# Experts of a mixture layer: gate and up columns in two passes with the gather between, sums after the next down products

## What is computed

```
logits = h @ router_w + router_b                 # 32 experts
top_vals, top_idx = top_k(logits, 4); gates = softmax(top_vals)
# per expert e, for the tokens that chose it:
gu   = x @ w_gu[e] + b_gu[e]                      # 1024 -> 2048: gate, up
gate = min(gu[:, :1024], 7);  up = clip(gu[:, 1024:], -7, 7)
y    = ((up + 1) * gate * sigmoid(1.702 * gate)) @ w_down[e] + b_down[e]
out[token] += gates[token, e] * y
```

## Time and profile before

| | us |
|---|---|
| three runs, median (lowest, highest) | 1225.59 (1220.59, 1228.70) |
| the profiled execution, its own time | 1226.34 |
| its span in the trace | 1224.4 |
| PE busy | 1032.1 (84%) |
| DVE, ACT, POOL busy | 378.8, 173.7, 127.2 |
| read from HBM | 455.56 MB |
| granted TensorE clock, mean | 0.95 |

### The profile page before, as it was taken

The page is one execution under the profiler, slowest core; times in us unless marked ns, Lnnn a source line. Parts: engine busy times, 40 slices in busy tenths (PEclk is TensorE's granted clock), DMA queues, the critical chain, the costliest instruction groups (busy, mean ns, idle before and its releaser), DMA issues.

```text
span 1224.4 us, 31651 instructions
## 1 busy us (share of the span) xinstructions
PE 1032.1 (84%) x11996; PEld 502.7 (41%) x11997; DVE 378.8 (31%) x1102; ACT 173.7 (14%) x459; POOL 127.2 (10%) x325
## 2 busy tenths in 40 slices
PE   5899988998999869898579899898765799989974
PEld 4678766646433314334123334333221233334331
DVE  1045592865222203223122231321211122222223
ACT  2242313142001001001000001000000010001002
POOL 0041103100101101001000010110100011000100
PEclk9899997997999989999879999999888899999998
DMA  9936937899999999999999995999999999999997
GB/s 340 338 138 226 351 94 201 319 312 393 384 426 427 427 429 428 428 428 429 428 429 429 428 400 216 429 429 429 428 428 428 430 428 429 428 429 429 428 428 298
DMA packets 77831, 463.68 MB, mean 379 GB/s; under 512 B 11531, under 2 KB 31185, under 8 KB 53146
## 3 DMA queue, kind: packets, MB, share of 16 engines
q1 hardware_dynamic: 70479, 460.88, 91.8%
q10 hardware_dynamic: 7315, 2.27, 0.9%
HBM read 455.56 MB, written 7.57 MB: 378 GB/s over the span
## 4 chain that ended last, share of the span: by engine, by line
PE 60%; DMA 17%; DVE 9%; SPq 6%; issue 5%; ACT 1%; DVEq 1%; ACTq 0%; POOLq 0%; POOL 0%
PE psum L655 26%; PE psum L671 13%; DMA weights<-in_w_gu 12%; PE psum L1011 4%; PE psum L630 3%; DMA work<-in_w_down 3%; SPq L898 3%; PE psum L1262 2%; PE psum L608 2%; PE psum L624 2%; DMA weights<-in_w_ada 2%; SPq L901 2%; PE psum L1016 2%; DVE work L2384 1%; PE psum L966 1%
## 5 line engine op out<-in xcount | busy, mean ns | idle before, releaser
L655 PE MATMUL psum<-weights,work 128*32 128x512 f32 x2928 | 357.1, 628 | 94.9 <-DMA weights<-in_w_gu 59.0
L655 PEld LDWEIGHTS psum<-weights,work 128*32 128x32 f32 x2928 | 93.1, 113 | 325.0 <-issue 237.2
L2384 DVE STREAM_TRANSPOSE work<-psum 128x256 f32<-128x256 f32 x53 | 23.9, 450 | 562.8 <-PE psum L655 562.8
L671 PE MATMUL psum<-weights,work 128*32 128x256 f32 x2624 | 152.8, 381 | 21.5 <-ACT work L1812 19.8
L671 PEld LDWEIGHTS psum<-weights,work 128*32 128x32 f32 x2624 | 80.4, 110 | 87.0 <-issue 35.2
L608 PE MATMUL psum<-work 128*32 128x257 f32 (+3 forms) x1296 | 91.5, 397 | 1.1 <-ACT work L1755 1.1
L1807 ACT ACTIVATE work<-work x53 | 22.1, 416 | 493.3 <-DVE work L2388 478.2
L1011 PE MATMUL psum<-work,weights 128*128 128x288 f32 x320 | 81.7, 412 | 0.0
L608 PEld LDWEIGHTS psum<-work 128*32 128x32 f32 (+1 forms) x1296 | 38.8, 112 | 70.8 <-issue 61.2
L1011 PEld LDWEIGHTS psum<-work,weights 128*128 128x128 f32 x320 | 60.3, 192 | 17.9 <-issue 2.0
L655 PE MATMUL psum<-work 128*32 128x512 f32 x464 | 58.7, 624 | 6.6 <-DMA work<-in_w_gu 6.6
(11 more groups left out here) (404 smaller groups left out, 921.9 us busy)
## 6 DMA issues: line engine op xcount, KB each, us to landing
weights<-in_w_gu SPq DMA_DIRECT2D x112, 2048.0 KB, 35.1
weights<-in_w_down SPq DMA_DIRECT2D x48, 2048.0 KB, 37.1
work<-in_w_gu SPq DMA_DIRECT2D x16, 2048.0 KB, 33.3
work<-in_w_down SPq DMA_DIRECT2D x16, 2048.0 KB, 40.5
weights<-in_w_ada SPq DMA_DIRECT2D x12, 2048.0 KB, 12.4
weights<-in_w_in SPq DMA_DIRECT2D x6, 2048.0 KB, 13.2
weights<-in_w_out SPq DMA_DIRECT2D x2, 2048.0 KB, 8.0
out<-weights SPq DMA_DIRECT2D x8, 512.0 KB, 9.9
```

The lines of the kernel that those rows point to most:

```text
L655: last = mm(bank(GB)[SLOTS * n:SLOTS * n + SLOTS, :].rearrange("p (a x) -> p a x", a=4), xTm[:, k, :], gu[:, k % 2, n], start=k == 0, stop ...
L671: last = mm(bank(YB)[SLOTS * q:SLOTS * q + SLOTS, 0:QW], hT[:, k, :], dn[:, k % 4, QW * q:QW * q + QW], start=k == 0, stop=k == KT - 1)
L2384: v.transpose(features, of_slots[0]).then_inc(s["hid_step"], 1)
```

## The change

In the first loop the products are made in two passes over k: the 1024 gate columns into bank 2, then `gather(i + 1)`, then the 1024 up columns into bank 3 (`UB`). DVE takes the gate half as soon as `gate_ps` says so, transposes the first half of the gathered tokens once the up pass has read k-tiles 0 to 3 (`gu_read`), and does the second half after the up half's transpose. `gu_read` now counts in the up pass alone.

In the second loop the down products (into bank 2) come first and `scatter(i)` behind them. `scatter` reads a copy `y_st`, which DVE makes from `y_sb` after the transpose of `selT`; the copy has the place of `b_down_sb`, so the products of b_down with the gates are moved before the first expert's second loop. ACT copies the *next* round's `hid` to the fixed place before it evicts a round; the first round is there already, so the first down products wait for `hid` alone, and `hidc` goes.

```diff
+        hid_next = M.at(E0 + 1536, NB + 1, KT * SLOTS)
+        y_st = b_down_sb
...
-            XB, GB, YB = 0, 2, 3
+            XB, GB, UB, YB = 0, 2, 3, 2
...
                 pe.wait_ge(s["sel"], i)
+                pe.wait_ge(s["xTm"], i - 1)
                 pe.wait_ge(s["gslot"], i - 1)
                 gather_by(selA, GC).then_inc(s["xg_ps"], 1)
...
-                pe.wait_ge(s["y_sb"], i)
+                pe.wait_ge(s["y_st"], i)
...
+                    pe.wait_ge(s["y_sb"], first)
                     pe.wait_ge(s["xTa"], i)
-                    for k in range(KT):
-                        if k % 2 == 0:
-                            gu = slot_gu(landed(k // 2)).rearrange("p j (a n x) -> p j n a x", a=4, n=NQ)
-                        if k == KT // 2:
-                            pe.wait_ge(s["xTm"], i)
-                        for n in range(NQ):
-                            last = mm(bank(GB)[SLOTS * n:SLOTS * n + SLOTS, :].rearrange("p (a x) -> p a x", a=4), xTm[:, k, :],
-                                      gu[:, k % 2, n], start=k == 0, stop=k == KT - 1)
-                        if k in (1, 3, 5):
-                            last.then_inc(s["gu_read"], 1)
-                    last.then_inc(s["gu_ps"], 1)
-                    gather(i + 1)
+                    for part in range(2):
+                        out = bank((GB, UB)[part])
+                        for k in range(KT):
+                            if k % 2 == 0:
+                                at = landed(k // 2) if part == 0 else slot_of(r, k // 2)[0]
+                                gu = slot_gu(at).rearrange("p j (a n x) -> p j n a x", a=4, n=NQ)
+                            if part == 0 and k == KT // 2:
+                                pe.wait_ge(s["xTm"], i)
+                            for n in range(NQ):
+                                last = mm(out[SLOTS * n:SLOTS * n + SLOTS, 0:QW].rearrange("p (a x) -> p a x", a=2), xTm[:, k, :],
+                                          gu[:, k % 2, n, 2 * part:2 * part + 2], start=k == 0, stop=k == KT - 1)
+                            if part and k in (1, 3, 5):
+                                last.then_inc(s["gu_read"], 1)
+                        last.then_inc(s["gu_ps" if part else "gate_ps"], 1)
+                        if part == 0:
+                            gather(i + 1)
+
+                if of:
+                    bias_products()
 
                 with pe.Fori(first, end) as i:
 
-                    scatter(i)
-                    pe.wait_ge(s["hidc"], i)
+                    pe.wait_ge(s["y_sb"], i)
+                    pe.wait_ge(s["xTa"], end)
+                    pe.wait_ge(s["hid"], i)
...
                     last.then_inc(s["y_ps"], 1)
+                    scatter(i)
+
+            def bias_products():
...
+                    act.wait_ge(s["hid"], last)
+                    act.wait_ge(s["y_ps"], i)
+                    act.copy(hid_all[:, 0, :], hid_next[:, round_behind(i, first), :].rearrange("p r n -> p (r n)"))
                     act.wait_ge(s["xg_ps"], 1)
-                    act.wait_ge(s["y_ps"], i)
-                    fn(y_sb, bank(3)[:, 0:QW], ACT.Identity, scale=gslot[:, round_of(i, first)]).then_inc(s["y_sb"], 1)
+                    act.wait_ge(s["y_st"], i)
+                    fn(y_sb, bank(2)[:, 0:QW], ACT.Identity, scale=gslot[:, round_of(i, first)]).then_inc(s["y_sb"], 1)
...
-                    v.wait_ge(s["gu_ps"], i)
+                    v.wait_ge(s["gate_ps"], i + 1)
+                    v.wait_ge(s["y_sb"], first)
                     v.transpose(features, of_slots[0]).then_inc(s["hid_step"], 1)
                     v.wait_ge(s["hid_step"], i * 5 + 1)
                     tt(kept.rearrange("p (k t) -> p k t", k=KT), part, bias[0], ALU.add).then_inc(s["hid_step"], 1)
                     v.wait_ge(s["hid_step"], i * 5 + 2)
                     ts(kept, kept, LIMIT, None, ALU.min).then_inc(s["g_ready"], 1)
+                    v.wait_ge(s["xg_ps"], i + 1)
+                    v.wait_ge(s["gu_read"], i * 3 + 2)
+                    x_half(0).then_inc(s["xTa"], 1)
+                    v.wait_ge(s["gu_ps"], i)
                     v.transpose(features, of_slots[1]).then_inc(s["hid_step"], 1)
-                    v.wait_ge(s["xg_ps"], i + 1)
-                    x_transposes()
+                    x_half(1).then_inc(s["xTm"], 1)
...
+                    v.wait_ge(s["y_sb"], i + 1)
+                    v.tensor_copy(y_st, y_sb).then_inc(s["y_st"], 1)
```

More of the change, by code:

```diff
@@ L184 @@
  wout_in wpool_in x1 x1_st x2T_ps xT_ps xTm x_in xg_ps xn xn2 y_ps y_sb z_sb cur gslot rank_b selT bgu_in
- bguT ahead xTa hidc curb """.split()
+ bguT ahead xTa y_st curb """.split()
 def build(nc, x_prompt, x_sample, c_prompt, c_sample, state_pool, state_conv, state_ssm, w_ada, b_ada,
@@ L587, in round_of, with round_behind @@
             return bass.ds(r, 1)
+        def round_behind(i, first):
+            r = nc.s_assert_within(i - first + 1, 1, NB, skip_runtime_bounds_check_because="288 tokens are at most nine rounds of 32")
+            return bass.ds(r, 1)
         def slot_of(e, j):
@@ L623, in scatter @@
                     r = slice(SLOTS * q, SLOTS * q + SLOTS)
-                    last = mm(samples_out[r, :], selT[r, 0:SLOTS], y_sb[r, :], start=False, stop=end)
+                    last = mm(samples_out[r, :], selT[r, 0:SLOTS], y_st[r, :], start=False, stop=end)
                 if end:
@@ L629, in scatter @@
                         r = slice(SLOTS * q, SLOTS * q + SLOTS)
-                        last = mm(total(q, c), selT[r, SLOTS + P * c:SLOTS + P * c + P], y_sb[r, :], start=False, stop=end and c == 1)
+                        last = mm(total(q, c), selT[r, SLOTS + P * c:SLOTS + P * c + P], y_st[r, :], start=False, stop=end and c == 1)
                 last.then_inc(s["total_ps"], 1)
@@ L675, in expert @@
                     last.then_inc(s["y_ps"], 1)
+                    scatter(i)
+            def bias_products():
+                pe.wait_ge(s["gbT"], 1)
+                pe.wait_ge(s["rb_in"], 16 * NQ)
+                for c in range(2):
+                    for q in range(NQ):
+                        r = slice(NE * q, NE * q + NE)
+                        mm(total(q, c), gT[r, span(c)], b_down_sb[r, :], start=False, stop=False)
+                for q in range(NQ):
+                    r = slice(NE * q, NE * q + NE)
+                    mm(samples_out[r, :], gT[r, span(2)], b_down_sb[r, :], start=False, stop=False)
             pe.wait_ge(s["h2"], 3)
@@ L710, in experts_pe @@
             expert(0, 0, of_first)
-            pe.wait_ge(s["rb_in"], 16 * NQ)
-            for c in range(2):
-                for q in range(NQ):
-                    r = slice(NE * q, NE * q + NE)
-                    mm(total(q, c), gT[r, span(c)], b_down_sb[r, :], start=False, stop=False)
-            for q in range(NQ):
-                r = slice(NE * q, NE * q + NE)
-                mm(samples_out[r, :], gT[r, span(2)], b_down_sb[r, :], start=False, stop=False)
             for r in range(1, PERIOD):
@@ L2329, in _ @@
             v.wait_ge(s["bguT"], 1)
-            v.memset(y_sb, 0.0).then_inc(s["y_sb"], 1)
+            v.memset(y_sb, 0.0).then_inc(s["y_st"], 1)
             v.wait_ge(s["h2_ps"], 3)
```

18 lines of the change are left out of this document (9 added, 9 removed).

## The result

The changed kernel takes 1227.28 us (median of 18 runs, 1225.77 to 1232.86); the kernel before takes 1222.51 us (18 runs, 1220.16 to 1230.98) beside it. The ratio is 1.0038, interval 1.0027 to 1.0050: 4.8 us slower by the medians. That is inside the range of 1218 to 1234, but the forecast was 1.2 us faster, and the sign is wrong beyond the interval.

What follows compares the result with a forecast made beforehand. The experts' stage was taken as bound by its loads, so the end moves with the holes and the tail: -5.5 + 4.3 = -1.2 us, from the median 1225.6 to 1224.4 us; range 1218 to 1234.

Steps and rivals of the forecast that it cites:

- the sum of the holes: Dry times of the load stream around the first and five-round experts: 16.0 against 21.5 us, 5.5 us gained.
- the third hole: Load stream dry after 730, until the five-round expert's first w_down slot is free: 5.2 us instead of 15.0.
- the base: One profiled execution of the kernel before, 1226.34 us, supplied the rows; the forecast time started from the median, 1225.6 us.
- PE's stretch: PE's work from 631.32 to 756.03, through the five-round expert: starts 6.8 us late, gains 12.4 us.
- the place behind the third hole: Next expert's first w_gu slot: free at about 760.2, needed at 760.25, so nothing runs dry (0 to 1 us).
- the tail: After the last w_gu load: ACT begins 2.3 us later, the last sum adds 2.0; 4.3 us lost.
- The first hole: Load stream dry at the first expert's start: first reload 4.9 us later, 9.2 us dry instead of 4.3.
- PE's costs: PE's time per round: first loop 8.42 us instead of 9.38, second loop 5.14 instead of 6.18.
- The rival that the turns don't shorten: None of the eleven loop turns gains: +9.8 us, 1235.4 us; decides if a turn gains under 0.9 us; chance 0.15.
- The loop overhead: Jump back at the loop turns, taken as 0; at the other end 5.5 us over eleven turns.
- PE's start behind L: Next round's start after the load landing at 625.23 before: 8.05 us behind that load, 6.8 us late.
- The rival on the clock: Half clock behind the loads at PE's stretch and the tail: +7.1 us, 1231.5 us; chance 0.15.

Runs made afterwards that it cites:

- first expert in one pass: The changed kernel, but the first expert alone takes gate and up columns in one pass over k, gather behind: 1223.17 us, ratio 1.0000.
- both ends in one pass: The changed kernel with first and last expert in one pass, the last with its sum ahead of its down products: 1218.51 us, ratio 0.9964.
- passes alone: The kernel before with gate pass, gather, up pass, but its old second loop, down products in bank 3: 1230.35 us, ratio 1.0065.
- sums alone: The changed kernel with gate and up in one pass everywhere and DVE's old first-loop order, keeping the new second loop: 1220.19 us, ratio 0.9980.
- late reloads: The kernel before, its first three reloads waiting for all of the first expert's gate and up products: 1228.53 us, ratio 1.0042.
- sums, last expert as before: The changed kernel with one pass everywhere, DVE's old first-loop order, and the last expert's sum ahead of its down products: 1219.13 us, ratio 0.9966.
- last expert kept busy: The changed kernel with extra repeated gate products between the last expert's loads, which also waits for all gathered tokens: 1227.45 us, ratio 1.0041.

## Why the forecast was wrong, point by point

**The step that failed** is the sum of the holes: "5.5 us gained", with nothing lost behind the third. Measured from S against typical traces of before, the last w_gu load used comes only 0.2 us sooner (S + 892.2 for 892.4): the third hole ends 2.0 us sooner and the place behind it takes 1.7 of that back. With a tail near its forecast the sum is positive. Four terms make up the way from the forecast -1.2 to the +4.2 us of the traces:

- the base: its one trace was 2.4 us slow up to the end of the third hole;
- PE's stretch: it gains 10.45 us and not 12.4, 1.95 less, while it starts 0.8 us less late than summed, so 1.1 us;
- the place behind the third hole, taken at 0: 1.7 us;
- the tail: 0.2 us.

All traces, from S. The typical before is the mean of its three later traces; its first trace, which the sum was made from, stands apart.

| trace | first reload | L | third hole ends | tail | span - S | median, us over before |
|---|---|---|---|---|---|---|
| before, the sum's base | 3.0 | 320.6 | 451.4 | 25.0 | 919.8 | |
| before, three later traces | 2.6 | 320.1 | 449.05 | 25.0 | 917.4 | 0 |
| after, three traces | 8.1 | 325.5 | 447.1 | 29.5 | 921.6 | +4.8 |
| first expert in one pass | 2.7 | 320.1 | 442.8 | 29.9 | 918.3 | +0.6 |
| both ends in one pass | 3.7 | 321.4 | 443.1 | 25.3 | 913.8 | -4.0 |
| passes alone | 8.0 | 325.3 | 454.0 | 27.9 | 925.5 | +7.8 |
| sums alone | 3.1 | 320.9 | 446.3 | 26.3 | 916.4 | -2.4 |
| late reloads | 9.0 | 326.6 | 455.6 | 25.1 | 924.1 | +5.1 |
| sums, last expert as before | 3.5 | 320.9 | 446.2 | 25.2 | 916.0 | -4.3 |
| last expert kept busy | 8.2 | 325.6 | 448.6 | 28.0 | 921.5 | +5.2 |

**The whole, closed.** From the typical before to after: the third hole ends 2.0 us sooner, the place behind it, where the next expert's first w_gu slot comes free, takes about 1.7 back, and the tail costs 4.5. That is +4.2 us from S, and the medians say +4.8. The forecast had -5.5 and +4.3.

**The first hole: right.** Forecast: first reload 4.9 us later. It went 8.0 us after S instead of 3.0, and L came 4.8 us later than in the sum's base, 5.4 later than in typical traces. Late reloads shows that this lateness is carried to the end: 6.5 us at L, 6.5 at the third hole, 6.7 at the end.

**PE's costs: nearly right.** A first-loop round takes 725.67 - 717.20 = 8.47 us (forecast 8.42, have 9.38), a second-loop round 734.36 - 729.15 = 5.21 and, from the next on, 5.23 (forecast 5.14, 6.18 in the earlier trace rows). The timeline of after:

```profile
717.20 1.07 PE L667 MATMUL psum<-weights,work 128*32 128x256 f32 x16
...
725.67 1.07 PE L667 MATMUL psum<-weights,work 128*32 128x256 f32 x16
...
729.15 3.64 PE L688 MATMUL psum<-weights,work 128*32 128x256 f32 x64
...
734.36 3.66 PE L688 MATMUL psum<-weights,work 128*32 128x256 f32 x64
```

The down products were taken at half of gate and up, 3.5 us, with twice the matmuls per column not priced; here they hold PE for 732.72 - 729.15 = 3.57. The rival that the turns don't shorten did not occur: each gains 0.9 to 0.95 us.

**The loop overhead: the end of an expert was missed.** I took 0 for the jump back, and inside the loops that holds. Where the second loop ends, it doesn't:

```profile
651.61 3.66 PE L688 MATMUL psum<-weights,work 128*32 128x256 f32 x64
655.20 0.63 PE L632 MATMUL psum<-work 32*32 32x256 f32 x8
...
657.83 3.66 PE L667 MATMUL psum<-weights,work 128*32 128x256 f32 x64 [0.93 <-issue]
```

TensorE stands 0.93 us with nothing to wait for; in the kernel before the same place, where the down products stood last, shows 0.45 us. The other end of an expert in the stretch shows 1.43 us against 0.98. Together that is 0.9 us. The gain from the start of PE's stretch to the end of the third hole is 124.71 us (631.32 to 756.03) minus 114.26 (637.92 to 752.18) = 10.45 instead of 12.4. Of the 1.95 us missing, 0.9 is the ends, and most of the rest the turns (5 x 0.05 + 6 x 0.09 = 0.8). The rival on the turns named 11.1 us as the gain below which the change loses (12.4 - 1.2 is 11.2). The gain was below it, by mis-sized terms and not by the rival's mechanism.

**PE's start behind L: the term was nearly right, its base was not.** Forecast: 8.05 us after L and 6.8 us late. In the pair of traces it is 7.35 us after L and, from S, 6.0 us late (637.92 - 631.32 = 6.6, less 0.56 by which S is later). But the 6.09 us of the earlier trace rows are not what the kernel before does as a rule: the three later traces have 4.25 to 4.26. Against them the stretch starts 8.5 us late. The changed kernel has 7.35, 7.4 and 7.3 us in its three traces, so here the slow case is the rule. That one row made the base 1.8 us too slow, and with L 0.5 us late in the same trace the base's third hole ends 2.4 us late. The row could have been doubted when the sum was made: its own window showed a clock of 0.56, and one execution can't say how often that happens. The median of three runs that stood beside it, 1225.59, was high too: over 18 runs it is 1222.51.

**The place behind the third hole: the wrong end.** The prediction bounded the next expert's first w_gu slot at 0 to 1 us and took 0 ("free at about 760.2 and needed at 760.25"). The slot is free at 762.60, since the third hole ended 1.7 us later than summed (0.56 of it because S is later, which moves the need as well) and the end of the expert costs 0.5. The window from 760 to 770 shows 1.0 us lost; counted by the landings up to the last w_gu load used, it is 1.2 to 2.2 us in the three traces of after.

**The tail: right in size, partly by luck.** Forecast 4.3 us. It is 29.5 (29.2 to 29.65) against 25.0. Its two halves were off against each other. Timeline of after, for the earlier trace rows:

```profile
1197.18 1.94 PE L667 MATMUL psum<-weights,work 128*32 128x256 f32 x16 [2.96 <-DMA weights<-in_w_gu]
...
1206.83 3.55 PE L688 MATMUL psum<-weights,work 128*32 128x256 f32 x32 [2.12 <-DVE work L2428]
...
1212.76 0.47 ACT L1838 ACTIVATE work<-psum,work 128x256 f32<-128x256 f32 x1
...
1214.40 0.29 DVE L2441 COPY work<-work 128x256 f32<-128x256 f32 x1
...
1214.80 0.63 PE L632 MATMUL psum<-work 32*32 32x256 f32 x8 [0.98 <-DVE work L2441]
```

The down products start 9.65 us after the load (forecast 10.4), but they run at the half clock behind 2.12 us of waiting, so ACT evicts at 15.6 us (forecast 14.4, 12.1 before): +3.5 instead of +2.3. The last sum starts 2.04 us after the eviction (forecast 2.65, 0.57 before): +1.5 instead of +2.0. Some 0.5 us are hidden in the end.

**The rival on the clock.** "The clock stays low behind a load" was priced at full half-clock length in both places, +7.1 us. Neither place is that bad: 7.4 and 9.65 us instead of 11.6 and 14. But part of it is what happened. In all seven traces of kernels with two passes the products behind L take 1.93 or 1.94 us, the half clock. In the seven with one pass (four of before, sums alone, sums with the last expert as before, late reloads) it is full in four and low, for part or all of the stretch, in three. The Trainium skill, TensorE: Matmul & The Clock Gate, "What's actually happening", has the low clock as the default that activity lifts. These counts agree with it, since a gate pass is half the work per load; the kernel kept busy agrees in part, with the clock up at 1188 after the extra products but down again at 1196. That the half work per load is the cause of the seven is argued from the counts and not shown by a run. The clock's share at L can be estimated: at the full clock the changed kernel would start its next round 5.8 us after L by the forecast's own sum, so of the 3.1 us by which it starts later than before about 1.5 are the clock and 1.5 the order of the work.

**What stays open.** By the medians the late reloads cost 5.1 us and by their trace 6.7, which its interval allows. The two parts of the change add up by the medians and miss the whole by 2.9 us by the traces. And one trace of each edited kernel can't say how its clock falls in other executions.

## What to carry over

A kernel bound by its loads pays for PE only at its holes and at its two ends. When an order is changed for the compute-bound middle, keep the old order in the first and the last turn: here that turned 1.0038 into 0.9964. But ask of each part of a change what it brings: the new order of the sums alone, with the last expert as before and no second pass anywhere, gives 0.9966. The single traces have the passes 2.2 us ahead in the middle (913.8 against 916.0 from S); the medians show no gain from them. Making the last reader of a buffer later (here `gu_read` behind a second pass) is a loss as large as the delay where the stream is dry; in the run made for it nothing downstream returned it. And a sum whose result is 1 us, made of terms of 5 us on one execution, gives no sign: look first whether the base row is typical, above all if its clock is not full.

## What was not expected of the hardware

- The time up to the first expert's products varies by 10 us between executions of the same code (296.5 to 306.3 in fourteen traces), twice what the change costs. Measured from S, the span of the changed kernel is 921.5 to 921.8 in three traces and that of the kernel before 917.3 to 917.5 in three of four.
- The half clock can set in while the array is at work: in the kernel kept busy it fell from 1.00 (1188 to 1194) to 0.50 (1196 to 1198), behind an idle stretch of 2.1 us, although products and gather had been running since 1193.4 (the window between, 1194 to 1196, has 0.67).
- The run-time end of an expert's loops shows as 0.93 us of idle TensorE behind a sum and 0.45 us behind down products. A likely reason, not shown, is that 3.66 us of down products cover more of the sequencer's work than a sum's 1.7 us.
